# Forgetting attention's outputs in two products a key block instead of three, with the high and low values side by side

## The reference

```python
def fox_attention(q, k, v, log_f):     # q, k, v: (1, 512, 8, 64)
    c = cumsum(log_f, over tokens)
    s = q @ k^T * 64 ** -0.5 + c[query] - c[key]
    s = where(key <= query, s, -inf)
    p = softmax(s)
    return p @ v                       # (1, 512, 8 * 64)
```

## Time and profile before

| | |
|---|---|
| time, median of 3 runs | 1189.07 us (1186.98 to 1190.51) |
| profiled execution, its own time | 1188.42 us |
| its span in the profile | 1186.7 us |
| TensorE busy | 1160.1 us, 98% of the span |
| VectorE, ScalarE, GpSimd busy | 352.4, 454.6, 499.4 us |
| granted TensorE clock, mean | 0.998 of full |

### The profile page before, as it was taken

The page is one execution under the profiler, slowest core; times in us unless marked ns, Lnnn a source line. Parts: engine busy times, 40 slices in busy tenths (PEclk is TensorE's granted clock), DMA queues, the critical chain, the costliest instruction groups (busy, mean ns, idle before and its releaser), DMA issues.

```text
span 1186.7 us, 15254 instructions
## 1 busy us (share of the span) xinstructions
PE 1160.1 (98%) x5664; PEld 965.5 (81%) x5664; DVE 352.4 (30%) x718; ACT 454.6 (38%) x744; POOL 499.4 (42%) x227
## 2 busy tenths in 40 slices
PE   8999999999999999999899999899999999999998
PEld 7888888888888778787778988778888888888886
DVE  2221311310006274655545204544122131130003
ACT  6232332322126455454535545456423233231213
POOL 5354354354443542222325754256434435435441
PEclk9999999999999999999999999999999999999999
DMA  6323333332322222111223442233332333323232
GB/s 201 105 91 99 96 94 101 92 103 89 106 89 71 89 89 72 54 54 43 83 69 109 160 142 89 73 126 107 104 105 90 98 96 92 103 89 106 89 107 107
DMA packets 86141, 115.13 MB, mean 97 GB/s; under 512 B 8974, under 2 KB 54092, under 8 KB 86092
## 3 DMA queue, kind: packets, MB, share of 16 engines
q1 hardware_dynamic: 86000, 114.44, 29.7%
q10 hardware_dynamic: 92, 0.02, 0.0%
HBM read 112.34 MB, written 2.10 MB: 96 GB/s over the span
## 4 chain that ended last, share of the span: by engine, by line
PE 61%; issue 24%; POOL 11%; DVE 2%; DMA 1%; ACT 1%; POOLq 0%; SPq 0%; DVEq 0%
PE bank L1436 20%; PE bank L1440 20%; PE bank L1437 20%; POOL w_lo L588 10%; PE bank L1477 1%; DVE h L1073 1%; DMA raw<-in_ffn_w_gu 1%; DVE bank L1062 0%; PE bank L1513 0%; POOL q_hi L626 0%; POOL q_lo L626 0%; DVE tmp L1062 0%; DVE f_ms L1060 0%; ACT w_hi L644 0%; ACT xh L658 0%
## 5 line engine op out<-in xcount | busy, mean ns | idle before, releaser
L588 POOL TENSOR_TENSOR w_lo<-raw,w_hi 128x1024 fp32r<-128x1024 f32 x204 | 488.3, 2403 | 665.0 <-ACT w_hi L644 664.3
L1436 PE MATMUL bank<-xh,w_hi 128*128 128x512 f32 (+1 forms) x912 | 349.8, 384 | 2.7 <-POOL w_lo L588 2.0
L1437 PE MATMUL bank<-xh,w_lo 128*128 128x512 f32 (+1 forms) x912 | 348.3, 382 | 0.0
L1440 PE MATMUL bank<-xl,w_hi 128*128 128x512 f32 (+1 forms) x912 | 348.3, 382 | 0.0
L644 ACT ACTIVATE w_hi<-raw 128x1024 fp32r<-128x1024 f32 x204 | 213.3, 1057 | 349.5 <-DMA raw<-in_ffn_w_down 167.5
L1436 PEld LDWEIGHTS bank<-xh,w_hi 128*128 128x128 f32 x912 | 171.5, 188 | 36.6 <-POOL w_lo L588 2.6
L1440 PEld LDWEIGHTS bank<-xl,w_hi 128*128 128x128 f32 x912 | 171.4, 188 | 33.6
L1437 PEld LDWEIGHTS bank<-xh,w_lo 128*128 128x128 f32 x912 | 171.5, 188 | 32.0
L1436 PE MATMUL bank<-w_hi,mid_hi 128*128 128x512 f32 x352 | 137.3, 390 | 0.0
L1440 PE MATMUL bank<-w_lo,mid_hi 128*128 128x512 f32 x352 | 137.0, 389 | 0.0
L1437 PE MATMUL bank<-w_hi,mid_lo 128*128 128x512 f32 x352 | 136.9, 389 | 0.0
(11 more groups left out here) (232 smaller groups left out, 1211.6 us busy)
## 6 DMA issues: line engine op xcount, KB each, us to landing
raw<-in_ffn_w_gu SPq DMA_DIRECT2D x176, 256.0 KB, 2.9
raw<-in_ffn_w_down SPq DMA_DIRECT2D x88, 256.0 KB, 2.8
raw<-in_mix_w_in SPq DMA_DIRECT2D x48, 256.0 KB, 2.8
raw<-in_mem_w_kv SPq DMA_DIRECT2D x32, 256.0 KB, 3.1
raw<-in_mem_w_o SPq DMA_DIRECT2D x32, 256.0 KB, 2.9
raw<-in_mix_w_out SPq DMA_DIRECT2D x16, 256.0 KB, 3.0
raw<-in_mem_w_q SPq DMA_DIRECT2D x16, 256.0 KB, 2.9
h<-in_x SPq DMA_DIRECT2D x4, 512.0 KB, 5.3
```

Source lines behind the costliest of these rows:

```text
L588: gp.tensor_tensor(w_lo[:, n % SLOTS, :], raw[:, n % SLOTS, :], w_hi[:, n % SLOTS, :].bitcast(F32), ALU.subtract).then_inc(lo_ready, 1)
L1436: pe.matmul(dst, w[0], x[0], start=start, stop=False, skip_group_check=loose)
L1437: pe.matmul(dst, w[1], x[0], start=False, stop=False, skip_group_check=loose)
L1440: return pe.matmul(dst, w[0], x[1], start=False, stop=stop, skip_group_check=loose)
```

## The change

The high and the low values of a head stand side by side in one tile, `v_hl` (64 high columns, then 64 low ones). Two matmuls a key block, with `pt_hi` and with `pt_lo`, then give the high values' product in 64 rows of bank 3 and the low values' product in the other 64. The low by low product is computed too. ScalarE copies the rows of the other half into the head's rows of `fox_y` (same memory as `fox_lo`), VectorE adds the head's own half to it (`y_sum`), and one turn later, in turns 4h + 7, ScalarE rounds `fox_y` to `fox_hi` and VectorE subtracts for `fox_lo`. For even heads the head's own rows hold the high values' product.

```diff
--- before.py
+++ after.py
@@ -260,8 +260,8 @@
         k_hi_a = sb("k_hi_a", [P, 2, SEQ], F32R, at=shared + 102 * kib)
         k_hi_b = sb("k_hi_b", [P, 2, SEQ], F32R, at=shared + 60 * kib)
         k_lo = sb("k_lo", [P, 4, SEQ], F32R, at=shared + 72 * kib)
-        v_hi = sb("v_hi", [P, TC, FOX_W], F32R, at=shared + 32 * kib)
-        v_lo = sb("v_lo", [P, TC, FOX_W], F32R, at=shared + 40 * kib)
+        v_hl = sb("v_hl", [P, TC, FOX_H, P], F32R, at=shared + 32 * kib)
+        v_hi, v_lo = v_hl[:, :, :, 0:FOX_D], v_hl[:, :, :, FOX_D:P]
         gq = sb("gq", [P, 2, SEQ], at=shared + 48 * kib)
         gk = sb("gk", [P, 2, SEQ], at=shared + 52 * kib)
         gke = sb("gke", [P, 2, SEQ], at=shared + 56 * kib)
@@ -284,6 +284,9 @@
         reset = sb("reset", [P, SEQ], at=shared + 100 * kib)
 
         fox_hi, fox_lo = (t[:, :, :].rearrange("p (c e) n -> p c e n", e=2)[:, :, 0, :] for t in (q_hi, q_lo))
+
+        q_flat = sb("q_flat", [P, FOX_H, SEQ], at=shared + 16 * kib)
+        fox_y = q_flat[:, :, :].rearrange("p (c e) n -> p c e n", e=2)[:, :, 0, :]
 
         gla_o = sb("gla_o", [P, GLA_H, 2, SEQ], at=shared)
         gla_a = sb("gla_a", [P, 4, 2, SEQ], at=shared + 16 * kib)
@@ -374,6 +377,8 @@
         pv_done = sem("pv_done")
         y_h = sem("y_h")
         y_l = sem("y_l")
+        y_part = sem("y_part")
+        y_sum = sem("y_sum")
 
         ke_turned = sem("ke_turned")
         ke_saved = sem("ke_saved")
@@ -444,6 +449,9 @@
                 eng.wait_ge(pair_done, g)
             else:
                 eng.wait_ge(w_used, B_IN + KB * (g + 1))
+
+        def fox_rows_of(hd):
+            return slice(FOX_D * (hd % 2), FOX_D * (hd % 2 + 1))
 
         def key_hi(c):
             return (k_hi_a, k_hi_b)[c // 2][:, c % 2, :]
@@ -806,8 +814,10 @@
                     elif g in (2, 4):
                         wait_group(act, g, m)
                         act.wait_ge(hinv, 2)
-                        act.activation((v_hi if g == 2 else gv)[:, m, :], b[m][:, :], ACT.Copy,
-                                       scale=rinv_tok[:, m:m + 1]).then_inc(in_hi, 1)
+                        dst, src = gv[:, m, :], b[m][:, :]
+                        if g == 2:
+                            dst, src = v_hi[:, m, :, :], src.rearrange("p (h d) -> p h d", d=FOX_D)
+                        act.activation(dst, src, ACT.Copy, scale=rinv_tok[:, m:m + 1]).then_inc(in_hi, 1)
                     elif g == 5:
                         act.wait_ge(in_tmp, 12 + m + 1)
                         act.activation(gr[:, m, :], tmp[:, m, :], ACT.Silu).then_inc(in_hi, 1)
@@ -838,8 +848,17 @@
                         return
                     hd = FOX_UNITS[done][0]
                     act.wait_ge(pv_done, hd + 1)
-                    r = slice(FOX_D * (hd % 2), FOX_D * (hd % 2 + 1))
-                    act.activation(fox_hi[r, hd // 2, :], bank[3][r, :], ACT.Copy).then_inc(y_h, 1)
+                    r, other = fox_rows_of(hd), fox_rows_of(hd + 1)
+                    act.activation(fox_y[r, hd // 2, :], bank[3][other, :], ACT.Copy).then_inc(y_part, 1)
+
+                def round_rows(done):
+
+                    if not 0 <= done < N_FOX or FOX_UNITS[done][1] < TC - 1:
+                        return
+                    hd = FOX_UNITS[done][0]
+                    r = fox_rows_of(hd)
+                    act.wait_ge(y_sum, hd + 1)
+                    act.activation(fox_hi[r, hd // 2, :], fox_y[r, hd // 2, :], ACT.Copy).then_inc(y_h, 1)
 
                 for k in range(N_FOX + LATE + 2):
                     if k < N_FOX - 1 and k % TC == TC - 1:
@@ -862,6 +881,7 @@
                                        bank[2][:, 0:nk * P].rearrange("p (j n) -> p j n", n=P),
                                        ACT.Copy).then_inc(pt_h, 1)
                     output(k - LATE - 1)
+                    round_rows(k - LATE - 2)
                     if k == PAIR_TURN[1]:
                         in_evacuate(4, (0, 1))
                     if k == END_TURN[1]:
@@ -1147,9 +1167,19 @@
                     if not 0 <= done < N_FOX or FOX_UNITS[done][1] < TC - 1:
                         return
                     hd = FOX_UNITS[done][0]
-                    r, c = slice(FOX_D * (hd % 2), FOX_D * (hd % 2 + 1)), hd // 2
+                    r, c = fox_rows_of(hd), hd // 2
+                    dve.wait_ge(y_part, hd + 1)
+                    dve.tensor_tensor(fox_y[r, c, :], bank[3][r, :], fox_y[r, c, :],
+                                      ALU.add).then_inc(y_sum, 1)
+
+                def low_rows(done):
+
+                    if not 0 <= done < N_FOX or FOX_UNITS[done][1] < TC - 1:
+                        return
+                    hd = FOX_UNITS[done][0]
+                    r, c = fox_rows_of(hd), hd // 2
                     dve.wait_ge(y_h, hd + 1)
-                    dve.tensor_tensor(fox_lo[r, c, :], bank[3][r, :], fox_hi[r, c, :].bitcast(F32),
+                    dve.tensor_tensor(fox_lo[r, c, :], fox_y[r, c, :], fox_hi[r, c, :].bitcast(F32),
                                       ALU.subtract).then_inc(y_l, 1)
 
                 for k in range(N_FOX + LATE + 2):
@@ -1180,6 +1210,7 @@
                                           pt_hi[:, 0:nk, i * P:(i + 1) * P].bitcast(F32),
                                           ALU.subtract).then_inc(pt_l, 1)
                     output(k - LATE - 1)
+                    low_rows(k - LATE - 2)
                     for g in (3, 5):
                         if k == PAIR_TURN[g - 3]:
                             in_evacuate(g, (0, 1))
@@ -1295,9 +1326,10 @@
                                           ALU.subtract).then_inc(in_lo, 1)
                     elif g == 2:
                         dve.wait_ge(in_hi, 8 + m + 1)
-                        dve.scalar_tensor_tensor(out=v_lo[:, m, :], in0=b[m][:, :], scalar=rinv_tok[:, m:m + 1],
-                                                 in1=v_hi[:, m, :].bitcast(F32), op0=ALU.mult,
-                                                 op1=ALU.subtract).then_inc(in_lo, 1)
+                        dve.scalar_tensor_tensor(out=v_lo[:, m, :, :],
+                                                 in0=b[m][:, :].rearrange("p (h d) -> p h d", d=FOX_D),
+                                                 scalar=rinv_tok[:, m:m + 1], in1=v_hi[:, m, :, :].bitcast(F32),
+                                                 op0=ALU.mult, op1=ALU.subtract).then_inc(in_lo, 1)
 
             def decayed(j):
 
@@ -1721,14 +1753,15 @@
                     hd = FOX_UNITS[done][0]
                     pe.wait_ge(pt_l, done + 1)
                     if hd:
-                        pe.wait_ge(y_l, hd)
+                        pe.wait_ge(y_sum, hd)
                     else:
                         pe.wait_ge(pt_zero, 2)
                     for j in range(TC):
-                        c, q0 = hd // 2, min(j, 2) * P
-                        last = three(bank[3][:, q0:SEQ],
-                                     (v_hi[:, j, c * P:(c + 1) * P], v_lo[:, j, c * P:(c + 1) * P]),
-                                     (pt_hi[:, j, q0:SEQ], pt_lo[:, j, q0:SEQ]), j == 0, j == TC - 1, True)
+                        q0 = min(j, 2) * P
+                        for pt in (pt_hi, pt_lo):
+                            last = pe.matmul(bank[3][:, q0:SEQ], v_hl[:, j, hd, :], pt[:, j, q0:SEQ],
+                                             start=j == 0 and pt is pt_hi, stop=j == TC - 1 and pt is pt_lo,
+                                             skip_group_check=True)
                     last.then_inc(pv_done, 1)
 
                 for k in range(N_FOX + LATE + 1):
@@ -1881,7 +1914,7 @@
                         last = pe.transpose(bank[t][:, j * P:(j + 1) * P], gke[:, c, m * P:(m + 1) * P],
                                             ident[:, :])
                     last.then_inc(ke_turned, 1)
-                pe.wait_ge(y_l, Y_FOX)
+                pe.wait_ge(y_sum, Y_FOX)
                 warm_up(bank[2], 1)
                 scores(0)
                 chunk_state(0)
```

## The result

The changed kernel takes 1193.35 us (median of 7 runs, 1191.67 to 1195.98), the kernel before beside it 1188.91 us (7 runs, 1186.98 to 1190.51). The ratio is 1.0036 with a 95% interval of 1.0023 to 1.0049: 2.7 to 5.8 us slower, where the forecast was 1192.3 us and 3.3 us slower. The prediction's bound for "no change", 0.3% or 3.6 us, lies inside that interval, so which side of the bound the change is on stays open. That it is slower is clear. The profiled execution of the changed kernel took 1195.98 us with a span of 1194.3 us; that is the slowest of the seven, so I compare stretches of it and not its span.

What follows compares the result with a forecast made beforehand. TensorE, busy 98% of the span, was taken to bound the kernel. -5.15 us saved, +7.80 lost in heads 0 to 5 and +0.63 at the end gave +3.3 us, 1192.3 us; range 1186.0 to 1195.8.

Steps and rivals of the forecast that it cites:

- The saving: TensorE's head outputs: four of twelve matmuls go, saving 0.64 us a head, 5.15 us for eight.
- The subtraction is held up by `w_lo` behind heads 0, 2, 4 and 5: VectorE's new subtraction waits for GpSimd; the next instruction starts 0.5 us behind `w_lo`; losses 0.91, 2.21, 1.56, 1.56 us.
- Heads 1 and 3 pay the plain length: No `w_lo` there; the maximum comes 0.90 us later, costing 0.90 us in head 1 and 0.66 in head 3.
- Head 2 pays its saving as well: Head 2's `pt_hi` chain doesn't move forward with its shorter output, so 0.64 us more is lost, 2.21 in all.
- Head 6 pays nothing, the end 0.63: Head 6: no maximum behind its subtraction, loss 0; at the end the first GLA scores start 0.63 us later.
- The copy at its old price: ScalarE's 64x512 copy out of the bank, now across partition halves, taken at 0.59 us, against 587 ns before.
- the same kind and 688 ns, so free: VectorE's addition of bank and SBUF replaces the subtraction from the bank at the same 688 ns, adding nothing.
- The sum: Whole kernel: -5.15 saved, 7.80 lost in heads 0 to 5, 0.63 at the end, giving +3.3 us.
- all hidden (-4.5): Rival: all new work is hidden and only the end pays, -4.5 us, 1184.6 us; chance 0.14.
- Not held up (-2.3): Rival: `w_lo` doesn't hold up the subtraction; heads 1, 2, 3 and the end pay, -2.3 us, 1186.8 us; chance 0.20.
- Held up behind heads 1 and 3 too (+6.4): Rival: `w_lo` also covers heads 1 and 3's subtractions, each paying 1.57 us more, +6.4 us, 1195.5 us; chance 0.12.

Runs made afterwards that it cites:

- e1: Changed kernel with two products kept but the old output path, low values' product left out of the result; 1184.01 us, ratio 0.9972.
- e2: Changed kernel with the subtraction of heads 0 to 6 reading bank 3 instead of `fox_y`, so one SBUF input; 1186.24 us, ratio 0.9988.
- e3: Changed kernel with the subtraction of heads 0 to 6 cut to 32 of 512 columns, still two SBUF inputs; 1189.24 us, ratio 1.0014.
- e6: Changed kernel with three products a key block again and the new output path kept; 1197.49 us, ratio 1.0082.
- e9: Changed kernel with late roundings and subtractions in turns chosen per head, the sum rounded ahead of the weight block; 1183.45 us, ratio 0.9963.
- e10: Changed kernel with the turn's weight block rounded behind the sum, so `w_lo` starts after the subtraction; 1191.36 us, ratio 1.0023.
- e4: Changed kernel with rounding and subtraction of heads 0 to 6 three turns later, in turn 4h + 10; 1186.98 us, ratio 0.9995.
- e5: Changed kernel with rounding and subtraction moved to a turn chosen for each head, head 7's behind the GLA copies; 1184.62 us, ratio 0.9978.
- e7: The changed kernel itself, run and profiled again ten times; 1191.60 us, ratio 1.0033.

## Why the prediction was right, point by point

- **The saving**: 0.64 us a head forecast; an output is 0.65 shorter in the trace, and the steps of e1's shift are 0.63 to 0.66. Right, and e1 shows it alone. (The 5.12 of the table is 8 x 0.64, not a measurement of its own.)
- **The subtraction is held up by `w_lo` behind heads 0, 2, 4 and 5**: right, those four lasted 2.06, 2.18, 2.19 and 2.05 us, the other four 0.69. e2 and e3 show the cause (the two SBUF inputs), which the prediction had only from the earlier trace rows. The maximum comes 0.47, 0.47, 0.48 and 0.58 us behind `w_lo`, for 0.5.
- **Heads 1 and 3 pay the plain length**: right in kind. The maximum of head 1 is 1.03 us later behind `pt_hi` and not 0.90, as the subtraction starts 0.03 later than put and the instruction behind it 0.72 us after it where I had 0.62. The place was wrong for head 1: not the wait at its transposition grew (1.02 us before and after) but the one at the `fill` matmul ahead of it, for `tmp`, which the prediction had left out; both wait for the same late VectorE, so the sum is near. That is luck in part.
- **Head 2 pays its saving as well**: right; 0.61 us of head 2's 2.09 is lost at the three-block transposition, ahead of the subtraction, and e6, which has no saving to lose, pays 1.64 for head 2 where the changed kernel pays 2.09.
- **Head 6 pays nothing, the end 0.63**: right, 0.03 and 0.70.
- **The copy at its old price, and "the same kind and 688 ns, so free"**: the step that was too low. The sum of the losses is 9.18 for 8.43. Of the 0.75 too little the copy and the addition seem to make most: e9 has them and hides the rest, and is 0.49 short of e1 (at the transposition where it arises, 0.13 more than e1 behind head 0, 0.17 behind head 2, 0.25 behind head 4). Their durations were forecast to 6 ns; what I had not priced is the spacing around the copy, which the last section shows for head 4; behind heads 0 and 2 it is argued from the same difference.
- **The sum**: +3.3 forecast, +4.06 in the stretch, +4.4 between the medians and 2.7 to 5.8 by the interval. Of the waits for `pt_lo` 7.8 more were forecast; 7.0 came, and 1.04 for `tmp`. The forecast time lies 1.05 us under the measured median. The measured ratio lies above the bound of 0.3% and the forecast below it, and the interval holds both.

The rivals: all hidden (-4.5) is refuted by the 7 us of waits, though e9, at -4.14, is that rival made true by another order. Not held up (-2.3) is refuted by the long subtractions; e2, which takes the condition away, gives -1.20. Held up behind heads 1 and 3 too (+6.4) did not come: GpSimd started after these subtractions, by 3.8 us behind head 1 (497.19 against 493.42) and by 2.6 behind head 3 (528.21 against 525.63).

## What to carry to other kernels

Work taken off the bounding engine paid nearly in full here (4.63 of 5.12 us), but what replaces it on the other engines must be placed by the slack of each turn, not by the engines' average load: the same instructions cost 8.7 us one turn behind the output and 0.5 us where the chain had cover. Before adding a VectorE instruction, look which GpSimd instruction runs there. If one does, and the new instruction has two SBUF inputs, make one come from a bank (e2) or move it (e9). And check what stands next in the line, since the hold-up passes to it (e10): the normalisation, with its single SBUF input, is held up too, so counting inputs alone isn't enough.

## What the runs showed of the hardware that was not expected

**A copy of the same duration that takes more of ScalarE's time.** Timeline of ScalarE behind head 4's output, the kernel before and the kernel after:
```profile
531.18 0.28 ACT L861 ACTIVATE pt_hi<-bank 128x128 fp32r<-128x128 f32 x1 [2.92 <-PE bank L1713]
531.36 0.58 ACT L842 ACTIVATE q_hi<-bank 64x512 fp32r<-64x512 f32 x1
531.84 1.25 ACT L809 ACTIVATE gv<-bank,rinv_tok 128x512 f32<-128x512 f32 x2
```
```profile
534.70 0.28 ACT L880 ACTIVATE pt_hi<-bank 128x128 fp32r<-128x128 f32 x1 [2.20 <-PE bank L1745]
535.00 0.60 ACT L852 ACTIVATE q_flat<-bank 64x512 f32<-64x512 f32 x1
535.62 1.27 ACT L820 ACTIVATE gv<-bank,rinv_tok 128x512 f32<-128x512 f32 x2
```
The old copy starts 0.18 us behind `pt_hi` and its successor 0.48 behind it: it overlaps both neighbours. The new one starts 0.30 behind and its successor 0.62: it overlaps neither, 0.26 us in all, and TensorE's next three-block transposition is late by 0.25 to 0.30 in every kernel with this copy but e10 (where the weight block ahead of it has moved and it comes 0.21 early) and by 0.00 in e1. ScalarE's work from `gv` to the `pt_hi` that it waits for stands 0.27 to 0.29 later, behind the same first transposition, in e9 than in e1. The copy changed in two ways at once, the halves and the type it writes. The kernel before speaks against the type: ScalarE's next copy out of a bank there (`cum_b`, 128x512, written as float32 too) starts at 532.98, 0.11 us before `gv` ends, and the `exp` behind it starts 0.12 before `cum_b` ends. That leaves the halves, but no run has one of the two changes alone.

**The normalisation waits for GpSimd as the subtraction does**, 2.62 to 2.66 us in place of 0.49 (e10, four times), with a single SBUF input. (The Trainium skill, "SBUF — State Buffer", section Who interferes with whom, counts `tensor_scalar` among the operations that can take the pair shared with GpSimd; the row agrees.)

**TensorE's clock behind the GLA scores falls in some executions.** Windows of the kernel before, then of the kernel after, around the same matmuls (they begin at 590.36 and at 596.11); the column behind POOL is the granted clock:
```profile
588.00:590.00 2.00, 0.84 (x16) 0.70 (x14) 0.48 (x1) 1.78 (x4) 0.00 (x0) 1.00 0.00 0
590.00:592.00 2.00, 1.64 (x7) 1.41 (x8) 2.00 (x4) 0.96 (x2) 0.00 (x0) 1.00 0.00 0
```
```profile
594.00:596.00 2.00, 0.59 (x12) 0.46 (x10) 0.73 (x2) 1.78 (x4) 0.00 (x0) 1.00 0.00 0
596.00:598.00 2.00, 1.89 (x5) 1.54 (x6) 1.76 (x3) 0.71 (x2) 0.00 (x0) 0.52 0.00 0
598.00:600.00 2.00, 2.00 (x7) 1.62 (x6) 0.00 (x0) 0.00 (x0) 0.00 (x0) 0.62 0.00 0
```
In the kernel after TensorE pauses 1.51 us and then runs at about the lower level, 1.2 GHz: its 512-column matmuls are 0.43 us apart instead of 0.23. From the first of them to the first transposition of `mem_n` it takes 6.85 us where the other level gives 5.27. The clock fell so in both profiles of the changed kernel and in e1, e2, e4 and e5; it did not in both of the kernel before, nor in e3, e6, e9 and e10. What TensorE does ahead of it doesn't tell these apart: in all twelve profiles the first of these matmuls comes 16.00 to 16.01 us behind the first GLA scores, after a pause of 1.51 or 1.52 us. Nor does the kernel: a fall of this size takes 0.0014 off the mean clock of an execution (an estimate, from the windows 0.52 and 0.62 in a span of 1194.3 us), and two of e7's ten executions of the changed kernel have a mean of 1.000, as have two of e2's eleven and one of twelve each of e4 and e5. That fits the timed ratios, which show no whole 1.6 us that goes with the change: the changed kernel's (1.0036, 1.0033) are worth 4.3 and 3.9 us, which the stretch has without it. What decides it in an execution stays open.
